# Half-size products in cross-attention, a shorter routing chain, and another order of expert loads

## The reference, cut to what matters

```
for layer in range(2):
    h = h + hybrid_mixer(rmsnorm(h), ...)                 # ends with  y @ w_mix_out
    h = h + memory_cross_attention(rmsnorm(h), rmsnorm(mem), w_xq, w_xkv, w_xo)
                                                          # q = xn @ w_xq ; k, v = split(memn @ w_xkv)
    h = h + (swiglu if layer == 0 else moe_swiglu)(rmsnorm(h), ...)

def moe_swiglu(xn, w_router, w_gate, w_up, w_down):
    logits = xn @ w_router                                # 8 experts
    top_vals, top_idx = lax.top_k(logits, 2); top_w = softmax(top_vals)
    y = sum over e of combine[:, e] * ((silu(xn @ w_gate[e]) * (xn @ w_up[e])) @ w_down[e])
```

## Time and profile before

| what | value |
| --- | --- |
| median of 3 runs | 2622.48 us (2619.43 to 2625.99) |
| the profiled execution | 2621.56 us |
| its span, first to last instruction | 2619.7 us |
| TensorE busy | 96% of the span |
| VectorE, ScalarE, GpSimd busy | 39%, 17%, 6% |
| mean granted TensorE clock | 0.988 of full speed |

### The profile page before, as it was taken

The page is one execution under the profiler, slowest core; times in us unless marked ns, Lnnn a source line. Parts: engine busy times, 40 slices in busy tenths (PEclk is TensorE's granted clock), DMA queues, the critical chain, the costliest instruction groups (busy, mean ns, idle before and its releaser), DMA issues. The chain is left out here.

```text
span 2619.7 us, 79230 instructions
## 1 busy us (share of the span) xinstructions
PE 2512.5 (96%) x35723; PEld 2149.0 (82%) x35723; DVE 1018.2 (39%) x2501; ACT 446.0 (17%) x1045; POOL 149.9 (6%) x205
## 2 busy tenths in 40 slices
PE   8999999999989999999999999899999999999998
PEld 6888878778879989999999898677768688877775
DVE  4612554461220010110101102456673478775676
ACT  2101000210132322000000001410010445442000
POOL 0100000010012222000000000000000000000000
PEclk9999999999979999999999999999999999999999
DMA  7544554544569999999999999426654000020443
GB/s 233 162 129 131 175 160 148 163 160 145 197 262 407 407 407 406 372 408 407 408 407 407 407 407 298 136 65 205 219 188 129 3 7 7 7 69 23 163 165 123
DMA packets 290149, 571.31 MB, mean 218 GB/s; under 512 B 17678, under 2 KB 180500, under 8 KB 290020
## 3 DMA queue, kind: packets, MB, share of 16 engines
q1 hardware_dynamic: 290020, 569.49, 59.8%
HBM read 568.37 MB, written 5.28 MB: 219 GB/s over the span
## 5 line engine op out<-in xcount | busy, mean ns | idle before, releaser
L2472 PE MATMUL ps<-xg,ring 128*64 128x80 f32 x14336 | 511.8, 234 | 3.9 <-issue 0.7
L2472 PEld LDWEIGHTS ps<-xg,ring 128*64 128x64 f32 x14336 | 502.9, 137 | 11.1 <-DMA ring<-in_moe_w_up_dram 5.7
L2593 DVE TENSOR_TENSOR hidden<-acted,ps 128x320 f32<-128x320 f32 x64 | 28.5, 446 | 665.0 <-PE ps L2472 665.0
L2488 PE MATMUL ps<-hidden,expert_down 128*64 128x80 f32 x7168 | 259.9, 234 | 11.1 <-DMA expert_down<-in_moe_w_down_dram 5.6
L2488 PEld LDWEIGHTS ps<-hidden,expert_down 128*64 128x64 f32 x7168 | 253.1, 138 | 15.7 <-issue 8.4
L631 PE MATMUL ps<-xT,ring 128*128 128x256 f32 (+1 forms) x848 | 189.5, 384 | 3.0 <-PEq L474 3.0
L631 PEld LDWEIGHTS ps<-xT,ring 128*128 128x128 f32 (+1 forms) x848 | 156.3, 186 | 33.0 <-issue 3.5
L631 PE MATMUL ps<-ring,xT 128*128 128x256 f32 (+1 forms) x800 | 164.9, 367 | 4.1 <-PEq L1136 2.2
L631 PEld LDWEIGHTS ps<-ring,xT 128*128 128x128 f32 x800 | 144.4, 190 | 24.4 <-issue 6.4
L2530 ACT ACTIVATE ring<-second 128x1792 f32<-128x1792 f32 x44 | 74.8, 1699 | 151.4 <-PE ps L2472 133.3
L1883 PEld LDWEIGHTS ps<-xT,ring 128*128 128x128 f32 x720 | 87.1, 192 | 15.7 <-issue 8.8
(11 more groups left out here) (518 smaller groups left out, 3675.1 us busy)
## 6 DMA issues: line engine op xcount, KB each, us to landing
expert_down<-in_moe_w_down_dram SPq DMA_DIRECT2D x96, 1024.0 KB, 17.1
ring<-in_moe_w_gate_dram SPq DMA_DIRECT2D x84, 896.0 KB, 16.2
ring<-in_moe_w_up_dram SPq DMA_DIRECT2D x84, 896.0 KB, 16.7
ring<-in_mlp_w_dram SPq DMA_DIRECT2D x64, 1024.0 KB, 5.5
second<-in_moe_w_gate_dram SPq DMA_DIRECT2D x22, 1792.0 KB, 16.9
second<-in_moe_w_up_dram SPq DMA_DIRECT2D x22, 1792.0 KB, 17.7
ring<-in_w_xkv_dram SPq DMA_DIRECT2D x16, 1024.0 KB, 5.4
expert_down<-in_moe_w_down_dram SPq DMA_DIRECT2D x32, 512.0 KB, 16.5
```

The lines of the kernel that those rows point to most:

```text
L2472: mm = pe.matmul(bank[b][o:o + HEAD, at, :], w[:, c, f * P + o:f * P + o + HEAD], xg[:, p * E_STEP + c, :], start=(p == 0 and c == 0 and a ...
L2488: mm = pe.matmul(yT[c // 4][o:o + HEAD, c % 4, :], w[:, j, c * P + o:c * P + o + HEAD], hidden[:, f, :], start=False, stop=False, skip_gro ...
L2593: dve.tensor_tensor(hidden[:, part, :], acted[:, part, :], src, ALU.mult).then_inc(hidden_ready, 1)
```

## The change

1. `rows_values_queries` is written anew. The first piece and the last one stay whole. Each of the ten between becomes seven products of half size, each four matmuls of 128x128 by 128 columns. VectorE makes four sums of a piece's blocks one piece ahead, four sums of each left or right operand (three times in all), and joins each piece's products in five operations; for `h` it adds the joined result, for `v` and `qT` ScalarE copies it.
2. `route` gets shorter: the list of items is made on 15 partitions at once, the picks of the first item come straight from the ranks, and the first gather, the turn of `pick_w` and the clearing of the sums run inside this block, beside the making of the list.
3. `FIRST` is 4 in place of 3, and from the eleventh chunk (`BEFORE_UP = 10`) the load of the down weights goes out between the gate and the up weights of the next chunk.
4. The last item is written out apart from the loop: its close gathers, clears and turns nothing.

```
-        OUT, VALUES = 8, 8
-            jobs = self.rows_jobs(x, 0, h, True) + self.rows_jobs(memory_g, 4, v, False)
-            for p in range(4):
-                jobs += self.cols_jobs(x, 8 + p, 2, qT, 2 * p)
...
+                        product(one[b][:, 0, :], a11, b11)
+                        product(one[b][:, 1, :], a12, b21)
+                        pe.wait_ge(sums_ready.sem, sums_ready.at(p))
+                        pe.wait_ge(sums_of_x.sem, sums_of_x.at(p // 4 + 1))
+                        product(two[b][:, 3, :], a22, T[:, T3])
+                        product(two[b][:, 0, :], S[:, S1], T[:, T0])
+                        product(two[b][:, 1, :], S[:, S3], T[:, T2])
+                        product(one[b][:, 2, :], S[:, S2], T[:, T1])
+                        product(two[b][:, 2, :], S[:, S4], b22).then_inc(done.sem, 1)
...
+                    left_sums(X_rows, left_of(x), sums_of_x)
+                    sums_of_weights(1)
+                    for p in range(PIECES - 1):
+                        if 1 <= p < PIECES - 2:
+                            sums_of_weights(p + 1)
+                        if p == 1:
+                            left_sums(X_memory, left_of(memory_g), sums_of_x)
...
+                        join(p)
...
+                        if p == TURN_AFTER + 1:
+                            right_sums(X_rows, right_of(x), sums_of_x)
...
-                link(tt(match[:], key[:].unsqueeze(1).to_broadcast([1, K, V]), k_no[:], ALU.is_equal))
-                for n, no in enumerate((e_no, v_no)):
-                    link(tt(pickv[:], match[:], no[:].unsqueeze(1).to_broadcast([1, K, V]), ALU.mult))
-                    link(dve.tensor_reduce(found[:, n, :], pickv[:], AX_X, ALU.add))
+                for t in range(TT):
+                    ts(pick[:, t, :], slot_from_one[:], rank[:, t, 0:1], None, ALU.is_equal)
+                    ins = ts(pick_w[:, t, :], slot_from_one[:], rank[:, t, 0:1], wts[:, t, 0:1], ALU.is_equal, ALU.mult)
+                ins.then_inc(self.pick_ready.sem, 1)
+                link(dve.tensor_tensor_scan(upto[:], self.ones[0:K, 0:V], active[:], 0.0, ALU.mult, ALU.add))
+                link(tt(key[:], upto[:], active[:], ALU.mult))
+                link(stt(chosen_numbers[:], key[:].unsqueeze(1).to_broadcast([K, 2, V]), item_no[:, 0:1], numbers[:], ALU.is_equal, ALU.mult))
+                dve.tensor_reduce(found[:], chosen_numbers[:], AX_X, ALU.add).then_inc(found_ready.sem, 1)
...
-        FIRST = 3
+        FIRST, BEFORE_UP = 4, 10
...
                 for g in range(1, MOVED + 1):
                     if g < MOVED:
-                        load_ahead(g + 1)
+                        load_ahead(0, g + 1)
+                        if g < BEFORE_UP:
+                            load_ahead(1, g + 1)
                     load_down(g)
+                    if BEFORE_UP <= g < MOVED:
+                        load_ahead(1, g + 1)
...
+                before_last = items_before_last(pe)
+                with pe.Fori(0, before_last) as i:
+                    chunks(i)
+                    close(i, False)
+                chunks(before_last)
+                close(before_last, True)
```

More of the change, by code:

```diff
@@ L1417, in tensor @@
[L1417 to L1430, removed]
@@ L1457, in rows_values_queries @@
+        run.taken += PIECES
+        self.vec_step.over(chain.n)
+        for signal, n in ((self.squares_summed, TT), (self.pool_step, TT), (rstd, TT), (scaled, TT), (turned, KC), (by_vector, KC // 2), (by_scalar, KC // 2),
+                          (done, PIECES + 1), (joined, PIECES - 2), (sums_ready, PIECES - 2), (sums_of_x, 3), (self.evac_dve, len(OUT)), (self.evac_act, 9)):
             signal.over(n)
@@ L1463, in cross_attention @@
             qT = self.tmp(ctx, "qT", [P, KC, SEQ])
-            self.rows_values_queries(l, memory_g, v, qT, bias_work)
+            with ExitStack() as inner:
+                if l:
+                    flat = self.expert_down[:].rearrange("p a b -> p (a b)")
+                    spare = self.second[:, 3 * UNIT:4 * UNIT]
+                else:
+                    flat, spare = self.tmp(inner, "sums", [P, 3 * UNIT + D])[:], self.tmp(inner, "sums_memory", [P, UNIT])[:]
+                parts = [flat[:, k * UNIT:(k + 1) * UNIT].rearrange("p (k a s) -> p k a s", k=4, a=KC // 2) for k in range(3)]
+                made = flat[:, 3 * UNIT:3 * UNIT + D].rearrange("p (a s) -> p a s", a=8)
+                scratch = (parts[0:2], parts[2], spare.rearrange("p (k a s) -> p k a s", k=4, a=KC // 2), made)
+                self.rows_values_queries(l, memory_g, v, qT, bias_work, scratch)
             self.attend(XH, self.xT, XD ** -0.5,
@@ L2201, in route @@
+    def route(self, ctx, rows, table, items, n_items, slot_no, picks):
         I, ps = self.I, self.ps
@@ L2452, in turn_pick, with chunks @@
                     mm.then_inc(pick_turned, 1)
-                pe.wait_ge(zeros_ready, 1)
-                clear()
-                pe.wait_ge(pick_ready, 1)
-                gather()
-                pe.wait_ge(xg_ready, 2)
-                turn_pick()
-                count = items(pe)
-                with pe.Fori(0, count) as i:
+                def chunks(i):
                     with pe.Fori(0, n) as k:
@@ L2490, in _, with close @@
                             mm.then_inc(down_done, 1)
-                    pe.wait_ge(pick_ready, i + 2)
-                    pe.wait_ge(pickT_ready, i + 1)
-                    gather()
+                def close(i, last):
+                    if not last:
+                        pe.wait_ge(pick_ready, i + 2)
+                        pe.wait_ge(pickT_ready, i + 1)
+                        self.gather_rows(pe, rows, pick, xb)
+                    else:
+                        pe.wait_ge(pickT_ready, i + 1)
                     for half in range(2):
@@ L2555, in _, with chunks @@
                             move_gate(g, E_PIECES - 1)
-                    close(i)
-                with act.Fori(FIRST, count) as i:
+                    close(i, False)
+                def chunks(i):
                     with act.Fori(0, n) as k:
                         activate(i * n + k)
-                    close(i)
+                with act.Fori(FIRST, before_last) as i:
+                    chunks(i)
+                    close(i, False)
+                chunks(before_last)
+                close(before_last, True)
             @block.vector
@@ L2572, in make_pick, with item @@
                     ins.then_inc(pick_ready, 1)
[L2574 to L2587 removed]
+                def item(i, last):
+                    if not last:
+                        make_pick(bass.ds(i + 1, 1), i + 1)
                     with dve.Fori(0, n) as k:
@@ L2603, in _ @@
                             dve.tensor_tensor(d, d, ps[:, 6 + t, :], ALU.add).then_inc(added, 1)
+                    if not last:
+                        dve.wait_ge(pick_turned, i + 2)
+                        dve.tensor_copy(pickT[:], tb).then_inc(pickT_ready, 1)
+                before_last = items_before_last(dve)
+                with dve.Fori(0, before_last) as i:
+                    item(i, False)
+                item(before_last, True)
     def bias_rows(self, ctx):
```

375 lines of the change are left out of this document (261 added, 114 removed).

## The result

The changed kernel takes 2590.97 us (median of 4 runs, 2588.94 to 2591.94); the kernel before, run beside it, 2622.71 us. The ratio is 0.9878, 95% interval [0.9862, 0.9894]: 31.7 us less. The forecast was 2594.7 us.

The account below looks back on a forecast made before the run. TensorE was taken to bound the projections, VectorE's chain routing, and the transfer stream at 407 GB/s the experts' end. Gains 12.8 + 6.8 + 5.6 + 2.6 = 27.8 us gave 2593.8, as median 2594.7 us; range 2588 to 2605.

Parts of the forecast that it names:

- Part 1: Projections of both layers: ten half-product pieces each take 6.26 us in place of 6.90, saving 12.8 us in all.
- The turning: Projections, after the sixth piece: VectorE's tightest place; sums ready 0.7 us into the first query piece, wanted at 1.8, no stall.
- Part 2: Routing: shorter selection and early gather start the first expert product 6.8 us sooner; bounds 4.5 and 7.5 us.
- The clearing: Routing: clearing the sums moves to where TensorE waits for the chosen experts; it costs 1.1 us if uncovered.
- The rival of the clock: First expert chunk: the clock stays low, up to 6.8 us more at half speed, 3.4 us lost, 2598 us; chance 0.08.
- All of it passes to the end: Routing's whole 6.8 us reaches the end, since the transfer stream restarts when TensorE frees its first pieces.
- Part 3: Expert loads: a fourth item ahead closes the 5.7 us hole at the third close; 5.6 us taken, bounds 3 and 5.7.
- Over that item the stream falls back by 108.2 - 102.2 = 6.0 us against TensorE: Fourth item loaded ahead: the stream's lag of 6.0 us exceeds the 5.7 us hole, so nothing of it is left.
- I cost it at nothing: Expert loads: putting down weights ahead of the next up weights was priced at 0 us.
- the hole only moves: Rival: the hole opens again at the fourth item's close, with 0.3 to 2 us to spare; 2600 us, chance 0.12.
- Part 4: Last close: combination 1.7 us sooner without the gather, next block 0.9 us sooner; 2.6 us, bounds 1.5 and 4.
- The new code: Last item: the loop body's second copy is new code for TensorE; its 3.8 us slack a chunk covers the fetch.

Follow-up runs that it names:

- number 9: Changed kernel with the item written apart standing ahead of the loop as the first item, and five items loaded ahead: 2589.8 us, ratio 0.9871.
- number 1: Kernel before with only the new half-size products; routing, loads and closes as before: 2608.78 us, ratio 0.995.
- number 2: Kernel before with only the new routing and the block after it; projections, loads and last close as before: 2614.74 us, ratio 0.9974.
- number 6: Changed kernel with three items loaded ahead and the old order of loads: 2595.51 us, ratio 0.9897.
- table of five: Changed kernel and four variants by items ahead and new order's start: 3/never 843.46, 4/never 841.55, 3/11th chunk 839.85, 4/11th 836.23, 3/5th 835.52 us of experts.
- number 10: Changed kernel with two more unused VectorE additions ahead of each half piece's sums: 2592.14 us.
- number 11: Changed kernel with four more unused VectorE additions ahead of each half piece's sums: 2614.15 us.
- number 7: Changed kernel with three items loaded ahead and the new order of loads from the fifth chunk: 2590.94 us, ratio 0.9881.
- number 4: Changed kernel with the last item back in the loop, so its close gathers, clears and turns again: 2595.99 us, ratio 0.9904.
- number 8: Changed kernel with the item written apart standing ahead of the loop as the first item, four items loaded ahead: 2590.08 us, ratio 0.9874.
- number 5: Changed kernel with four items loaded ahead but the old order of loads: 2597.3 us, ratio 0.9896.

## Why the prediction was right, and where it was not

**The sum.** The four parts were to give 27.8 us; the stages that they change give 13.07 + 6.55 + 5.27 + 2.56 = 27.45 us. The median is 3.7 us below the forecast. Of this, 1.4 us is the stage behind the experts, which was in no part; the other 2.3 us are within what unchanged stages differ by from one execution to another.

**Part 1: right.** 13.1 us against 12.8; one term, 6.26 us a piece, came from another stage's rows and held. VectorE's work on a piece of `h`, 5.2 us forecast, is 5.23. The turning was said to leave 1.1 us (sums ready 0.7 us into the piece, wanted at 1.8). In the changed kernel the first query piece starts at 181.88, its sums are ready at 182.05 + 0.69 = 182.74, 0.9 us in, and they are wanted at 183.66: 0.9 us are left. Timeline:

```profile
181.88 1.95 PE L1450 MATMUL ps<-xT,ring 128*128 128x128 f32 x16
182.05 0.69 DVE L1533 TENSOR_TENSOR sums<-ring,sums 128x512 f32<-128x512 f32 x1
183.66 1.06 PE L1450 MATMUL ps<-sums,ring 128*128 128x128 f32 x8
```

Work added to the earlier pieces finds more room, since VectorE is idle for 2.05 us before the join at 175.83. That is why two more sums a piece cost a wait of only 0.6 us and four 4.3: if the sums of three pieces lie on that path, the work added is 3.8 and 7.6 us, and both give 3.2 to 3.3 us of cover, an estimate, near the 2.05 + 0.92 us that the trace shows. A 128-column record every 0.112 us again, and no spacing by weight loads; the rule of the Trainium skill named in the prediction (TensorE: Matmul & The Clock Gate, Back-to-back issue gap), from whose figures the prediction estimated a cost of 61 us for this part, is not borne out here.

**Part 2: the path right; the size holds for this execution.** From the ranks to the first product 9.2 us were forecast, 9.29 measured. Selection was to end 1.5 us behind the ranks (1.25 measured), the gather 6.7 us (6.41); the rest was to take 2.5 us (2.88 measured, of which 2.69 are issue). Two errors of 0.3 to 0.4 us cancel. The clearing, priced at 1.1 us, takes 2.50 us at the lower clock and is covered as supposed. But the stage's 19.81 us are the longest of eleven kernels with this routing code: the other ten take 17.7 to 18.8 us, at a granted clock of 0.71 to 0.80 where this one has 0.61. Window of number 9, the shortest:

```profile
707.51:725.24 17.73, 12.78 (x132) 11.39 (x133) 10.84 (x54) 5.54 (x11) 2.68 (x13) 0.80 0.84 313
```

The old routing took 26.36 and 26.56 us (number 1). So the part is worth 6.6 us here and 7.6 to 8.8 us elsewhere, and a forecast right to 0.3 us owes that to this execution's clock. The rival of the clock did not come between these two profiles (first 448 products 18.30 and 18.10 us), but the same products take 15.71 us in number 1 and 17.0 to 17.4 in the other kernels with the new routing: what the clock does at this place differs by a few us between executions, and the prediction gave it 0.08 as a matter of the change alone. "All of it passes to the end" is not refuted. Numbers 2 and 6 have larger holes, but each has the clock drop described there, and it is of the same size; whether an earlier start adds anything was not tried.

**Part 3: the size right, the reason wrong.** The step that failed is this: "Over that item the stream falls back by 108.2 - 102.2 = 6.0 us against TensorE", and with it "I cost it at nothing" for the order. The 102.2 us were read from an item behind the hole. While two chunks are ahead in the old order, down weights come late, and an item takes 103.4 to 109.0 us, near the stream's own 108.2. The wait was there in the trace of before: its items 2 and 3, which I had not read. Timeline of the kernel before, the second item's last down products, then two gathers (third item 103.4 us):

```profile
943.78 9.58 PE L2488 MATMUL ps<-hidden,expert_down 128*64 128x80 f32 x224 [2.87 <-DMA expert_down<-in_moe_w_down_dram]
953.19 2.38 PE L136 MATMUL ps<-pick,rows 128*64 128x80 f32 x64
...
1056.58 2.39 PE L136 MATMUL ps<-pick,rows 128*64 128x80 f32 x64
```

The table of five gives each half its price, once the 1.6 us of clock are taken out of its first line (841.9 us) and numbers 10 and 11 (835.4 and 835.6 us) stand for the changed kernel; these are estimates. The order alone, one chunk of it, takes 2 us off the experts, the fourth item alone 0.3 us, both together 6.4 us (5.3 against the kernel before as measured). The fourth item is worth some 4.4 us beside the order, because only then do the items ahead run without waits, faster than the stream. The rival "the hole only moves" is what happens with the fourth item and the old order. And number 7 shows that the item count isn't the point: the same cover comes from sparing the waits of the second item.

**Part 4: right.** 2.56 us against 2.6. The new code was to be covered by 3.8 us a chunk; it costs 6.3 us in one chunk. The last item takes TensorE 102.24 + 6.26 = 108.5 us then, the stream 108.1 to 108.2: the cover of the four chunks is used up, and TensorE and no longer the transfers ends the item, as the missing wait shows. What this costs the end is 0 to 0.4 us, by numbers 4, 8 and 9 against 10 and 11. (A slip in the sum: the low ends give 2588.3 us, not 2588.5.)

**Not in the sum: the clock behind the close.** Windows of 5 us from the first matmul behind the last close: kernel before, changed kernel, number 10.

```profile
1598.23:1603.23 5.00, 5.00 (x24) 4.56 (x25) 4.00 (x6) 4.08 (x9) 0.18 (x1) 0.66 0.79 247
```

```profile
1572.09:1577.09 5.00, 5.00 (x31) 4.55 (x32) 3.97 (x6) 4.93 (x10) 0.19 (x1) 1.00 0.95 314
```

```profile
1570.41:1575.41 5.00, 5.00 (x24) 4.82 (x25) 4.06 (x6) 3.33 (x7) 0.20 (x1) 0.66 0.97 303
```

Numbers 7 and 10 have the short close too and drop to the lower level all the same (the stage then takes 70.57 and 70.71 us, not 69.03); numbers 2 and 4 have the full close and don't drop. So these 1.4 to 1.7 us do not follow from the close's length. What decides it stays open.

**The best version.** Numbers 7, 8 and 9 are 0.7 to 1.0 us shorter in the experts than the changed kernel's profile, and 0.4 us at most from numbers 10 and 11; no median is apart from the changed kernel's by more than its interval. None is shown to be better.

## What to carry to other kernels

When a load is issued further ahead, look at what is queued behind it: here the next chunk's up weights ahead of this chunk's down weights slowed TensorE to the stream's pace, and that, not the depth of the buffering, kept the hole open. Read the pace of an item from the items that run under the mode in question, waits in brackets included, not from a steady one later. A stage made faster may be priced by rows of another stage that already runs the same set of instructions; count the other engine's work a piece beside it, since cover of 1 us a piece is the difference between 1 and 12 us a stage. And before a difference of 1 or 2 us between two profiles is given a cause in the change, compare the same products under the same code in both: here one drop of the clock can pass for a deeper hole, and another for the price of new code.

## What the runs showed of the hardware

- Two more additions a piece on VectorE cost 0.9 us a stage, four cost 11.6: at 5.23 + 1.3 = 6.5 us of VectorE's work on a piece of `h`, against TensorE's 6.26, the stage hardly moves, at 5.23 + 2.5 = 7.8 us VectorE sets the pace there. Of the 11.6 us, 4.6 lie in five pieces that wait for their sums, and 7.0 in the first query piece, behind them: 4.3 us of wait and 2.6 us of products at a granted clock of 0.56 (192 to 198 us) after it.
- The first run of a second copy of the code cost TensorE 0.4 to 0.7 us once and then 1.56 to 1.85 us three times, about every 128 products (with their weight loads 256 instructions, 16 KB), 29.5 us for a chunk in place of 23.24, when the transfers are at 406 GB/s. It happened in every kernel with a second copy, at the same point of the copy, moved with the copy in numbers 8 and 9, and in no kernel without one. The first copy's own first run, in the changed kernel's first item, shows one such wait, 0.88 us; why it pays less was not tried. The Trainium skill (Runtime: NRT & Kernel Launch, Instruction fetch mechanics) says that code comes in blocks of 16 KB and that this is mostly hidden, behind the issue of instructions. The size agrees with the packets here; the hiding does not, for the second copy.
- Unchanged stages differ between executions by 1 to 5 us: in the profile of number 5 the 950 us behind the experts' next stage took 954.37 us, in the changed kernel's 949.08. Single drops of the granted clock are part of it: a 50 us window from 1693.5 has 0.97 in number 5 and 1.00 in the same place of the changed kernel. A drop costs 1.4 to 1.7 us at each of these places (the fourth item of numbers 2 and 6, the second of number 7, the stage behind the experts).
